# The first DMAs of a two-layer trunk: x's first columns moved from SP's queue to the head of ACT's

## What is computed

```python
def rms_norm(x, g):
    y = xf * lax.rsqrt(jnp.mean(xf * xf, axis=-1, keepdims=True) + RMS_EPS)
    return (y * g).astype(x.dtype)

for i in range(DEPTH):                     # DEPTH = 2
    hn = rms_norm(x, pre_norm_g[i])
    y = moba_mixer(hn, w_in, w_out) if i % 2 == 0 else conformer_mixer(...)
    x = x + rms_norm(y, post_norm_g[i])
```

## Time and profile before

| | us |
|---|---|
| median of 3 runs | 848.79 |
| lowest and highest of them | 847.62, 848.79 |
| the profiled execution | 849.06 |
| its span, first to last instruction | 847.3 |
| PE busy in the span | 837.2 (99%) |

### The profile page before, as it was taken

The page is one execution under the profiler, slowest core; times in us unless marked ns, Lnnn a source line. Parts: engine busy times, 40 slices in busy tenths (PEclk is TensorE's granted clock), DMA queues, the critical chain, the costliest instruction groups (busy, mean ns, idle before and its releaser), DMA issues.

```text
span 847.3 us, 12107 instructions
## 1 busy us (share of the span) xinstructions
PE 837.2 (99%) x3875; PEld 694.7 (82%) x3875; DVE 684.5 (81%) x1179; ACT 428.0 (51%) x592; POOL 336.3 (40%) x169
## 2 busy tenths in 40 slices
PE   9999999999999999999999999999999999999996
PEld 6888888888888888888888788888888888888884
DVE  4688799988999899968556629999999999566555
ACT  5744535464444634454445675544544464574441
POOL 0343005500540014400000398888888878772000
PEclk9999999999999999999999999999999999999998
DMA  9956656656567546646655365555555555566522
GB/s 314 315 157 207 184 153 192 193 162 196 156 188 220 176 149 190 206 155 229 212 192 190 116 206 193 198 174 175 197 186 171 188 163 196 188 217 236 194 97 99
DMA packets 97509, 159.49 MB, mean 188 GB/s; under 512 B 3300, under 2 KB 38468, under 8 KB 97092
## 3 DMA queue, kind: packets, MB, share of 16 engines
q1 hardware_dynamic: 97428, 159.04, 58.0%
q10 hardware_dynamic: 48, 0.02, 0.0%
HBM read 156.94 MB, written 2.10 MB: 188 GB/s over the span
## 4 chain that ended last, share of the span: by engine, by line
PE 98%; issue 1%; DMA 0%; DVE 0%; ACT 0%; DVEq 0%; POOLq 0%; POOL 0%; SPq 0%
PE acc L421 29%; PE acc L423 29%; PE acc L422 29%; PE X L431 2%; PE acc L406 1%; PE acc L408 1%; PE acc L407 1%; PE acc L487 1%; PE acc L502 1%; DMA xrow<-in_x 0%; PE X L563 0%; PE X L548 0%; PE X L547 0%; PE X L564 0%; PE X L562 0%
## 5 line engine op out<-in xcount | busy, mean ns | idle before, releaser
L776 ACT ACTIVATE w_hi<-raw 128x1024 fp32r<-128x1024 f32 x282 | 298.9, 1061 | 354.4 <-PE acc L423 354.0
L421 PE MATMUL acc<-w_hi,xT_hi 128*128 128x512 f32 x864 | 338.9, 392 | 0.0
L423 PE MATMUL acc<-w_hi,xT_lo 128*128 128x512 f32 x864 | 336.5, 389 | 0.0
L422 PE MATMUL acc<-w_lo,xT_hi 128*128 128x512 f32 x864 | 336.2, 389 | 0.0
L1061 DVE TENSOR_TENSOR w_lo<-raw,w_hi 128x1024 fp32r<-128x1024 f32 x182 | 245.7, 1366 | 78.9 <-ACT w_hi L776 76.6
L1520 POOL TENSOR_TENSOR w_lo<-raw,w_hi 128x1024 fp32r<-128x1024 f32 x100 | 243.0, 2437 | 49.0 <-ACT w_hi L776 48.8
L423 PEld LDWEIGHTS acc<-w_hi,xT_lo 128*128 128x128 f32 x864 | 162.2, 188 | 34.2
L421 PEld LDWEIGHTS acc<-w_hi,xT_hi 128*128 128x128 f32 x864 | 162.3, 188 | 33.1 <-DVE xT_lo L1080 0.3
L422 PEld LDWEIGHTS acc<-w_lo,xT_hi 128*128 128x128 f32 x864 | 162.3, 188 | 32.7
L1345 DVE SCALAR_TENSOR_TENSOR X<-u_pad,taps,X 128x256 f32<-128x256 f32 x464 | 182.6, 484 | 0.0
L1483 POOL TENSOR_TENSOR small<-small 128x1 f32<-128x1 f32 (+1 forms) x7 | 4.3, 617 | 231.4 <-DVE small L1291 124.2
(11 more groups left out here) (151 smaller groups left out, 754.5 us busy)
## 6 DMA issues: line engine op xcount, KB each, us to landing
raw<-in_w_in SPq DMA_DIRECT2D x78, 1024.0 KB, 5.3
raw<-in_w_in SPq DMA_DIRECT2D x66, 512.0 KB, 4.5
raw<-in_w_out SPq DMA_DIRECT2D x32, 1024.0 KB, 5.0
gpost<-in_post_g SPq DMA_DIRECT2D x2, 1024.0 KB, 4.7
xrow<-in_x SPq DMA_DIRECT2D x4, 256.0 KB, 5.6
raw<-in_w_in SPq DMA_DIRECT2D x4, 256.0 KB, 4.9
xrow<-in_x SPq DMA_DIRECT2D x2, 512.0 KB, 9.8
bout<-in_b_out SPq DMA_DIRECT2D x1, 1024.0 KB, 7.0
```

What stands on the lines that cost most here:

```text
L421: nc.tensor.matmul(a, hi[:, k, rows], w_hi[:, slot, i], start=(k == 0), stop=False)
L422: nc.tensor.matmul(a, hi[:, k, rows], w_lo[:, slot, i], start=False, stop=False)
L423: last = nc.tensor.matmul(a, lo[:, k, rows], w_hi[:, slot, i], start=False, stop=(k == KT - 1))
L776: nc.scalar.activation(w_hi[:, slot], raw[:, u % LOADS, 2 * half:2 * half + 2], ACT.Copy).then_inc(hi_ready[slot], 1)
```

## The change

The load of x columns 0 to 255 leaves SP's queue and becomes the first DMA of ACT's queue, ahead of the norm weights. SP's queue goes from the identity straight to weight tile 0. The semaphore, the destination and the size of the load stay as they are, and so do all instructions on PE, DVE and GpSimd.

```diff
             sp.dma_start(ident[:], identity).then_inc(ident_in, 16)
-            x_load(0, 0)
             w_load(0, 0, 0, tile_in[0])
             w_load(0, 1, 1, tile_in[1])
             x_load(1, 1)
...
+            act.dma_start(xrow[:, :, 0:SEQ], x.rearrange("b (m p) n -> p (b m) n", p=P)[:, :, 0:SEQ]
+                          ).then_inc(x_in[0], 16)
             act.dma_start(pre_rows[:], pre_g.rearrange("l (t c) -> (l t) c", c=P)).then_inc(pre_in, 16)
```

## The result

Over 15 runs of each, the changed kernel takes 849.81 us (848.98 to 850.52) and the kernel before 847.69 us (847.07 to 849.09). The medians differ by 2.1 us; the ratio estimated from all runs is 1.0021 with a 95% interval of 1.0014 to 1.0027, that is 1.2 to 2.3 us slower. The loss is clear, and lies about at the 0.2% that was called no change. The prediction was 849.4, a loss of 0.57 us. The sign holds, and so does the wait that was named, but the size of the loss was taken three to four times too small. That the time still comes within 0.4 us is luck: the median of before that it started from, 848.79, was 1.1 us too high, and the loss that was added 1.55 us too small.

The account below looks back on a forecast made before the run. PE was taken as the bound, one unbroken queue from start to tail. Transposes 1.03 us later, partly made up at the faster pace, leave 0.57 us: 848.79 + 0.57 = 849.4 us, range 847.6 to 850.6.

Parts of the forecast that it names:

- the wait that was named: PE's wait for the norm weights, landing at 4.85 behind x; x's transposes behind it start at 6.35 instead of 5.32.
- That the start moves the end: PE's work is one unbroken queue from start to tail; moving its beginning moves the end by as much.
- Norm weights behind x: On ACT's queue, the norm weights land right behind x, at 4.85; PE is free for x 1.5 us later.
- the upper bound: Latest landing of the norm weights on ACT's queue: 0.73 us behind x's 4.84, at 5.6.
- The start of before: In the kernel before, x landing at 5.28 sets its transposes' start at 5.32; the change makes that 1.03 us later.
- the stated turning point: The change turns from gain to loss when the norm weights land at 3.8 us.
- What of it reaches the end: Of the 1.03 us later start, 0.57 us remains at the end if PE's clock rises near 9.6 as now.
- the rise moves back with the start: Rival: PE's clock rise is delayed with x's transposes, so the whole 1.03 us remains, 849.8 us; chance 0.18.
- the forecast's own account: Norm weights late and clock rise near 9.6: a later start partly made up, loss 0.57 us; chance 0.50.
- Weights earlier at no cost: Weight tiles on SP's queue issued 0.45 to 0.47 us earlier, costed at nothing.
- the lower bound of 4.4: Earliest landing of x from ACT's queue; bounds 4.4 to 5.3, with 4.84 taken.
- The cover for tile 0: ACT finishes tile 0's high part at 6.64, before PE reaches the products at 7.29; landing after 6.6 would cost.

Follow-up runs that it names:

- e11: Kernel before with seven thrown-away matmuls ahead of the waits for identity and norm weights, none between them and x, timed a second time: 847.76 us, ratio 0.9997.
- e1: Kernel before, no edit, profiled a second time: 847.66 us.
- e10: Changed kernel, no edit, timed and profiled again: 850.25 us, ratio to before 1.0021.
- e2: Changed kernel with ACT's two DMAs exchanged, norm weights first and x second: 849.24 us, ratio to before 1.0014.
- e3: Changed kernel with ten thrown-away matmuls instead of four before PE's wait for the norm weights: 848.90 us, ratio to before 1.0013.
- e4: Changed kernel with the three thrown-away matmuls between norm weights and x moved ahead of the wait (seven, then none): 848.22 us, ratio to before 1.0007.
- e5: Kernel before with the norm weights moved from ACT's queue to SP's, right behind x's first columns: 848.99 us, ratio 1.0014.
- e6: Changed kernel with the norm weights on SP's queue behind the identity, x alone on ACT's: 849.17 us, ratio to before 1.0016.
- e7: Kernel before without the three thrown-away matmuls between the norm weights and x: 848.79 us, ratio 1.0011.
- e8: Kernel before with seven thrown-away matmuls ahead of the waits for identity and norm weights, none between them and x: 847.47 us, ratio 0.9996.
- e9: Kernel before with weight tile 0 on ACT's queue behind the norm weights, x still on SP's: 849.07 us, ratio 1.0008.

## Why the prediction was right in kind and wrong in size

The start of the twelve products of tiles 1 and 2 in the chain orders the profiles. Added to 838.9 it gives the execution's time within 0.1 us in all twelve profiles in which PE was not held up by the later loads, e11 being the exception (the pace is read from the timeline, as the first start from which it is near 0.23):

| kernel | x's transposes from | fast pace by | twelve products from | execution |
|---|---|---|---|---|
| before, first profile | 5.32 | 9.6 | 10.19 | 849.06 |
| before, e1 | 4.41 | 7.2 | 8.74 | 847.67 |
| after | 6.74 | 9.3 | 10.91 | 849.78 |
| after, e10 | 6.60 | 8.9 | 10.38 | 849.23 |
| e2, x second on ACT | 6.02 | 10.8 | 11.10 | 849.99 |
| e3, gap filled | 6.38 | 4.6 | 9.71 | 848.65 |
| e4, the three ahead | 5.90 | 6.1 | 9.28 | 848.22 |
| e5, norm weights late | 6.14 | 8.4 | 9.88 | 848.74 |
| e6, x alone on ACT | 5.71 | 10.5 | 10.74 | 849.65 |
| e7, without the three | 4.14 | 8.1 | 9.17 | 848.12 |
| e8, seven ahead | 4.87 | 9.7 | 9.97 | 848.84 |
| e9, tile 0 on ACT | 6.55 | 9.2 | 10.79 | 849.66 |

**That the start moves the end.** Right: that is what the constant 838.9 says. The loss lies wholly in the first 11 us. By it the medians of 849.81 and 847.69 belong to starts at 10.9 and 8.8, which are those of the profile after and of e1.

**Norm weights behind x.** Right in kind. They land 0.8 us behind x (after) and 1.05 (e10), where "right behind" was taken and 0.73 was the upper bound. As x came 0.5 us sooner than taken, the two errors nearly cancel, by luck: 5.14 against 4.85. The 1.5 us from the moment when PE takes them up to x's transposes held (5.24, PE's load for the norm transpose, to 6.74). e4, which takes the three matmuls off this path and keeps PE busy longer ahead of it, has 0.4 of the 2.1 us left. The rule that the prediction cites from the Trainium skill (DMA: Bandwidth & Descriptors, "Queues, rings and completion order") has the semaphore's write wait for the earlier writes of its DMA engine across that engine's queues; the prediction left the last words out and applied the rule to one queue. The order of landing agrees with it: the norm weights land behind x in all four profiles of the changed order (4.3 and 5.1 after, 4.6 and 5.4 in e3, 4.8 and 5.6 in e4, 3.9 and 5.0 in e10), and in e6, with the two on different queues, too (3.9 and 4.1). That it is this write which waits, and not the transfer itself which is slow, no run here shows.

**The start of before.** This is the term that was taken too small. "The transposes start at 6.35 instead of 5.32: 1.03 us later" rested on one execution in which x landed 4.1 us after its issue. In the other profiles with x first on SP and the weights behind it, it took 2.8 (e1), 2.9 (e7), 3.1 (e11), 3.2 (e5) and 3.6 us (e8). In e1, the one of these whose time is that of the median of before, PE's own queue sets the start, at 4.41. The delay is 6.74 - 4.41 = 2.33 us, 1.3 more than the term in the sum. It also moves the stated turning point: the change loses as soon as the norm weights land after 2.9, not after 3.8. The chain named x as the last of the two, by 0.9 us only. There was a warning: the profiled execution, 849.06, was slower than all three runs of before, and 1.4 us slower than the lowest, while the prediction looked only at the 0.27 us to their median.

**What of it reaches the end.** Also too low, by the same baseline. "If the clock rises at the same moment as now" did not happen against the usual execution: 7.2 in e1, 9.3 and 8.9 after. With the start 2.33 and the rise 2.1 us later (after, against e1), nearly the whole delay remains, 10.91 - 8.74 = 2.17 us; in e10 the start is 2.19 and the rise 1.7 us later, and 1.64 remain. In kind this is the rival "the rise moves back with the start", which had 0.18; its 849.8 is the time measured only because its +1.03 was added to a median that was too high. Against the first profile of before the forecast's own account comes out: a start 1.42 us later, a rise at about the same moment, and 10.91 - 10.19 = 0.72 us left.

**Weights earlier at no cost.** Incomplete. In the changed kernel x starts 0.45 us ahead of tile 0 and landed at 3.9 to 4.8 in its four profiles (after, e3, e4, e10), in two of them below the lower bound of 4.4; but in the order of before it landed at 4.0 to 4.8 too (with one 5.28), so the earlier issue bought little. The cover for tile 0 was thinner than read: the 7.29 of the chain is not the first start of the products, which is 6.79 in the timeline of before, 0.15 behind the high part at 6.64. Where x and tile 0 start together, it lands at 5.98 (e2) and 6.50 (e9). And with x beside SP's queue what SP issues first comes late: with the norm weights taken from behind x, 1.3 of the 2.1 us remain (e6). The costs do not add up (1.1 in e5, 1.3 in e6, 1.4 in e2), since each acts on the same start. The prediction cites the Trainium skill (DMA: Bandwidth & Descriptors, "Issuing engines are not separate DMA queues") for saving only issue time with a second issuing engine. The traces agree in that no more than these 0.45 us of issue was gained, but that was the smaller half: the order in which the loads arrive is lost too.

**Still open.** What fixes the moment of the rise within a kernel. e8 and e11 are the same kernel with the fast pace at 9.7 and before 6; e4 rose across a gap of 1.6 us and e6, with 1.4, only by 10.5. The timed runs of e3 and e7 say that filling the gap pays and opening one costs, about 1 us each, but what decides a single execution is not shown. In the profile of e8 x came 0.5 us later than in that of e11, and PE stood still for 0.46 us before it; whether this is the cause is not shown either.

## What to carry to other kernels

Where one core waits for several first loads in turn, price each against the instruction that waits for it: 16 KB that PE takes first are more urgent than 256 KB that it takes 1.5 us later. Here a queue that holds the loads in order of need was worth more than the 0.45 us that a second issuer saves. Before a forecast of less than 1% is made from a profile, ask how far the profiled execution lies from the fastest run, and what in its first waits would be different there.

## What the hardware showed unexpectedly

A 256 KB load issued at 1.2 us behind only the identity landed after 2.8 to 4.1 us with the weight loads queued behind it, and after 5.3 us (e9) with one of them on the other queue. A 16 KB load issued behind 256 KB on the same queue landed 0.8 to 1.05 us after it on ACT's queue and 0.2 us after it on SP's (e5). The 64 KB identity, issued first of all on SP, took 1.8 to 2.2 us without x on the other queue and 2.5 to 3.4 us with x at the head of ACT's (e6, after, e3, e4, e10). The granted clock column read 1.00 in the stretches of the first 30 us while 512 columns were 0.41 us apart (the 1.2 GHz level) and while they were 0.23 apart (2.4 GHz); only the distance of the starts shows the level here. The moment at which it changed differed by over 3 us between two executions of one kernel (e8, e11).
